# Another order for the opening of a two-layer hybrid backbone on one core

## The reference

```python
mod_l = (jax.nn.silu(c) @ w_mod[l] + b_mod[l])[:, None, :]
mod_c = (jax.nn.silu(c_ctx) @ w_mod[l] + b_mod[l])[None, None, :]
sh1, sc1, g1, sh2, sc2, g2 = jnp.split(mod_l, 6, axis=-1)
hl = modulate(rms_norm(x, norm1[l]), sh1, sc1)
hc = modulate(rms_norm(xc, norm1[l]), sh1c, sc1c)
zl = split_cols(hl @ w_in)
...
scores = jnp.einsum('bhid,bhjd->bhij', qi, ki) * decay
```

## Time and profile before

| | us |
|---|---|
| median of 3 runs | 2636.76 |
| lowest and highest | 2631.75 and 2640.86 |
| profiled execution, own time | 2634.51 |
| its span | 2632.7 |
| PE busy | 2535.3 (96%) |
| POOL busy | 1482.3 (56%) |
| DVE busy | 1365.4 (52%) |
| ACT busy | 766.4 (29%) |

### The profile page before, as it was taken

One profiled execution on the slowest core, in us unless ns is written; L12 is line 12 of the kernel. 1 busy time (PEld: TensorE's weight loads), 2 busy tenths in 40 slices (PEclk: granted clock), 3 DMA queues, 4 the chain that ended last, 5 costly groups with the idle time before them and its releaser, 6 DMA issues.

```text
span 2632.7 us, 37897 instructions
## 1 busy us (share of the span) xinstructions
PE 2535.3 (96%) x15420; PEld 2108.4 (80%) x15420; DVE 1365.4 (52%) x1855; ACT 766.4 (29%) x1292; POOL 1482.3 (56%) x1375
## 2 busy tenths in 40 slices
PE   5999999999999999999999999998999999999998
PEld 2888888877777888888887889897778678888877
DVE  3632267643477867555565364327754777421241
ACT  4611333432355521111120033123432564211110
POOL 3443557523423536666669616556834445688896
PEclk8999999999999999999999999999999999999999
DMA  7342422312312833443434354222321247333332
GB/s 275 91 136 93 116 59 71 85 51 83 87 56 77 285 106 119 128 124 116 124 105 120 112 170 143 77 57 77 85 57 53 72 127 226 113 96 96 88 94 82
DMA packets 378211, 285.11 MB, mean 108 GB/s; under 512 B 10309, under 2 KB 338729, under 8 KB 377526
## 3 DMA queue, kind: packets, MB, share of 16 engines
q1 hardware_dynamic: 375744, 279.81, 35.4%
q10 hardware_dynamic: 1686, 2.78, 0.3%
q0 software_dynamic: 608, 0.09, 0.0%
HBM read 253.28 MB, written 29.36 MB: 107 GB/s over the span
## 4 chain that ended last, share of the span: by engine, by line
PE 84%; DVE 6%; POOL 4%; ACT 2%; issue 1%; DMA 1%; ACTq 0%; SPq 0%; DVEq 0%; POOLq 0%
PE ps L561 19%; PE ps L563 18%; PE ps L562 18%; PE ps L1272 3%; PE ps L774 3%; POOL w_lo L1426 2%; PE ps L610 2%; PE ps L1204 2%; PE ps L611 2%; PE ps L612 2%; PE ps L858 2%; PE ps L878 2%; POOL w_hi L1423 1%; PE ps L984 1%; PE ps L805 1%
## 5 line engine op out<-in xcount | busy, mean ns | idle before, releaser
L1423 POOL TENSOR_TENSOR w_hi<-ring,tiny 128x512 fp32r<-128x512 f32 x480 | 536.6, 1118 | 942.0 <-PE ps L563 559.0
L1426 POOL TENSOR_TENSOR w_lo<-ring,w_hi 128x512 fp32r<-128x512 f32 (+1 forms) x568 | 798.1, 1408 | 126.4 <-ACT w_hi L1653 88.8
L561 PE MATMUL ps<-hh,w_hi 128*128 128x512 f32 (+1 forms) x2320 | 839.7, 362 | 15.4 <-DVE hl L2155 10.4
L562 PE MATMUL ps<-hl,w_hi 128*128 128x512 f32 (+1 forms) x2320 | 818.1, 353 | 0.0
L563 PE MATMUL ps<-hh,w_lo 128*128 128x512 f32 (+1 forms) x2320 | 817.4, 352 | 0.0
L561 PEld LDWEIGHTS ps<-hh,w_hi 128*128 128x128 f32 x2320 | 441.0, 190 | 107.8 <-issue 26.3
L563 PEld LDWEIGHTS ps<-hh,w_lo 128*128 128x128 f32 x2320 | 441.0, 190 | 60.8
L562 PEld LDWEIGHTS ps<-hl,w_hi 128*128 128x128 f32 x2320 | 441.9, 190 | 55.3
L1958 ACT ACTIVATE arena<-ps,vec 128x768 f32<-128x768 f32 (+1 forms) x44 | 39.0, 887 | 424.8 <-PE ps L563 424.8
L1772 ACT ACTIVATE arena<-ps,tiny,vec 128x768 f32<-128x768 f32 (+1 forms) x120 | 108.6, 906 | 184.0 <-DVE tiny L2333 183.9
L2609 DVE SCALAR_TENSOR_TENSOR arena<-ps,vec,arena 128x511 f32<-128x511 f32 x66 | 43.6, 660 | 220.5 <-ACT arena L1958 219.7
(11 more groups left out here) (274 smaller groups left out, 3814.4 us busy)
## 6 DMA issues: line engine op xcount, KB each, us to landing
ring<-in_w_in SPq DMA_DIRECT2D x118, 512.0 KB, 4.0
ring<-in_w_mod SPq DMA_DIRECT2D x96, 512.0 KB, 3.9
ring<-in_w_up SPq DMA_DIRECT2D x88, 512.0 KB, 4.2
ring<-in_w_down SPq DMA_DIRECT2D x48, 512.0 KB, 3.6
ring<-in_w_out SPq DMA_DIRECT2D x32, 512.0 KB, 3.7
logits<-arena SPq DMA_DIRECT2D x32, 384.0 KB, 2.6
arena<-logits SPq DMA_DIRECT2D x32, 384.0 KB, 4.5
ring<-in_w_down SPq DMA_DIRECT2D x24, 384.0 KB, 3.2
```

The source lines that it names most:

```text
L561: pe.matmul(acc, wh[:, offset + k], hi[:, n, x:y], start=n == 0, stop=False)
L562: pe.matmul(acc, wh[:, offset + k], lo[:, n, x:y], start=False, stop=False)
L1423: pool.tensor_tensor(wh[:, 0:count], w, one[:].unsqueeze(2).to_broadcast([P, count, P]), ALU.mult).then_inc(*up("w_lead", ("lead", key, j)))
L1426: pool.tensor_tensor(wl[:, 0:count], w, wh[:, 0:count].bitcast(F32), ALU.subtract).then_inc(*up("w_split", ("split", key, j)))
```

## The change

It changes the order of the opening and of the retention branch of layer 0, and nothing that is computed:

1. ACT computes the conditioning vectors before it squares the tokens. One load of an activation table falls away with that.
2. PE multiplies the slices of groups 0 and 1 without a break, then turns `xn` 0 and 1, then group 2, the columns of groups 0 and 1, `xn` 2 and 3, group 3, the column of group 2, `xn` 4 to 7, and the column of group 3.
3. `f0` and `f1` are computed together (`opening_features`): for each operand tile PE first turns block `x` `k`, then multiplies the tile with the weights of both.
4. In the list of chunks `f1` follows `f0` at once, and the slices that stood between them come later.
5. DVE makes a rotation as soon as its feature tile is out, and strip 0 behind rotation 1, strip 1 behind rotation 2, strips 2 and 3 behind rotation 3. ACT takes the exponentials of strip 0 behind the copy of `f2`, those of strips 1, 2 and 3 behind the copy of `f3`.

```diff
 def slices_behind(l, b, slot):
     groups = columns_between(l)[b]
-    if b == "ret" and slot >= 3:
-        slot = {3: 2 * len(groups), 4: 3}.get(slot, slot)
+    if b == "ret":
+        slot = slot - 1 if slot > 0 else 2 * len(groups)
...
+            def opening_features(*places):
+                keys = [("f", 0, "ret", n) for n in range(2)]
+                for key, place in zip(keys, places):
+                    next_chunk(key)
+                    for s, n in room(key, *place):
+                        pe.wait_ge(s, n)
+                for k in range(KT):
+                    j, offset = k // (KT // 2), k % (KT // 2)
+                    turn_tokens("x", k)
+                    pe.wait_ge(*at(("hl", 0, 1, k)))
+                    for key in keys:
+                        pe.wait_ge(*at(("split", key, j)))
+                        for x, y in segs(T):
+                            mm = product(psum(key)[:, x:y], key, j, hh, hl, x, y, count=1, first=k, offset=offset)
...
                 if l == 0:
-                    for g in range(4):
+                    for g in range(2):
                         for kk in range(4):
                             modulation_slices(("msl", l, g, kk))
-                            if kk % 2 == 1:
-                                turn_tokens("xn", 2 * g + kk // 2)
...
+                    for k in range(2):
+                        turn_tokens("xn", k)
+                    for kk in range(4):
+                        modulation_slices(("msl", l, 2, kk))
+                    for g in range(2):
+                        modulation_turned(g)
+                    for k in range(2, 4):
+                        turn_tokens("xn", k)
+                    for kk in range(4):
+                        modulation_slices(("msl", l, 3, kk))
+                    modulation_turned(2)
+                    for k in range(4, KT):
+                        turn_tokens("xn", k)
                     modulation_turned(3)
...
+            conditions()
             for t in range(NT):
                 act.wait_ge(*at(("x_in", t)))
...
-                if t == 3:
-                    conditions()
...
-                        if l == 0 and b == "ret" and j < 4:
-                            strip_exponentials(l, j)
+                        if l == 0 and b == "ret" and 2 <= j <= 3:
+                            for h in ((0,), (1, 2, 3))[j - 2]:
+                                strip_exponentials(l, h)
...
                 if b == "ret":
                     for n in range(tiles):
                         turn_halves(n)
+                        for h in ((), (0,), (1,), (2, 3))[n] if l == 0 else ():
+                            strip_begun(l, h)
+                            strip_ended(l, h)
...
-                    if b == "ret" and l == 0:
-                        for h in range(4):
-                            strip_begun(l, h)
-                            strip_ended(l, h)
```

More of the change, by code:

```diff
@@ L563, in product @@
                     mm = pe.matmul(acc, wl[:, offset + k], hi[:, n, x:y], start=False, stop=n == whole - 1)
-                    if each and key == ("f", 0, "ret", 0):
-                        turn_tokens("x", n)
-                return mm
+                return mm
+            def opening_features(*places):
[12 more added lines that the diff above has]
+                            mm = product(psum(key)[:, x:y], key, j, hh, hl, x, y, count=1, first=k, offset=offset)
+                        if offset == KT // 2 - 1:
+                            mm.then_inc(*up("pe_half", ("half", key, j), *([("full", key)] if j else [])))
             def projection(key, hi, lo, width, banks, each=None):
@@ L1081, in behind, with banks @@
                         modulation_slices(key)
-                def banks(b):
+                def banks(b, j=None):
                     turn[0] += 1
+                    if l == 0 and b == "ret":
+                        return ((2, 3), (0, 1), (4, 5), (0, 1))[j]
                     return (0, 1) if turn[0] % 2 == (b != "ret" or l > 0) else (2, 3)
@@ L1093, in _ @@
                             each = None
-                            if b == "ret" and j == 0:
-                                each = lambda k: ("hl", l, 1, "first", k) if l else ("hl", l, 1, k)
+                            if b == "ret" and j == 0 and l > 0:
+                                each = lambda k: ("hl", l, 1, "first", k)
                             if b == "ret" and j == BR[b]["nq"] and l > 0:
@@ L1098, in _ @@
                             n = feature_order(b)[j]
-                            projection(("f", l, b, n), hh, hl, W[l] if is_q(b, n) else T, banks(b), each=each)
+                            if l > 0 or b != "ret" or j >= 2:
+                                projection(("f", l, b, n), hh, hl, W[l] if is_q(b, n) else T, banks(b, j), each=each)
+                            elif j == 0:
+                                opening_features(banks(b, 0), banks(b, 1))
                             if b == "ret" and j == 0 and l > 0:
@@ L2034, in decays_and_lambdas @@
                     link(dve.tensor_scalar(onorm[:, 1, l], onorm[:, 1, l], 1.0 - init, None, ALU.mult))
+            vectors_out(2)
+            vectors_out(3)
             for k in range(1, KT, 2):
@@ L2198, in norm, with strip_begun, strip_ended @@
                 rest(KT - 1)
+            def strip_begun(l, h):
+                D = dist[:, 0:NEAR]
+                dve.wait_ge(*at(("dist_in",)))
+                dve.tensor_scalar(e0, D, 0.0, lg[:, 8 * l + h:8 * l + h + 1], ALU.max, ALU.mult)
+                dve.tensor_scalar(e1, D, 0.0, lg[:, 8 * l + 4 + h:8 * l + 5 + h], ALU.min, ALU.mult).then_inc(
+                    *up("strip_in", ("strip_in", l, h)))
+            def strip_ended(l, h):
+                D = dist[:, 0:NEAR]
+                dve.wait_ge(*at(("strip_exp", l, h)))
+                link(dve.scalar_tensor_tensor(out=strip[:, h, 0:NEAR], in0=D, scalar=0.0, in1=e0, op0=ALU.is_ge, op1=ALU.mult))
+                link(dve.scalar_tensor_tensor(out=e1, in0=D, scalar=0.0, in1=e1, op0=ALU.is_le, op1=ALU.mult))
+                link(dve.tensor_tensor(strip[:, h, 0:NEAR], strip[:, h, 0:NEAR], e1, ALU.add))
+                link(dve.tensor_tensor(strip[:, h, NEAR:], strip[:, h, NEAR:], e2, ALU.add))
             def prep_tiles(l, b):
```

59 lines of the change are left out of this document (24 added, 35 removed).

## The result

The changed kernel takes **2645.51 us** (median of 11 runs, 2641.51 to 2656.20), the kernel before 2636.76 in the same series: ratio 1.0040, 95% interval 1.0027 to 1.0053. It is slower by about 9 us. Forecast was 2640, range 2630 to 2648: the time lies in the range, but on the upper side, and past the 0.3% (2644.7) that the forecast had drawn as the bound of "slower", to which it gave 0.21; the interval of the ratio includes that bound.

A forecast was written before the change was run, and what follows sets the result against it. PE, busy 96% of the span, was taken as the bound; 12.1 us won before `f2` are lost waiting behind the strips, plus 1.7 and 2.0 for the clock: 2636.76 + 3.7 is 2640 us, range 2630 to 2648.

The forecast's parts named there:

- slower: Whole kernel: measured time over 2644.7 us, beyond the 0.3% (7.9 us) told from no change; chance 0.21.
- the long stop: Second pair of value chunks: PE waits 13.8 us for ACT's copy of the values, plus 2.0 us for the fallen clock.

The follow-up runs named there:

- e1b: Changed kernel with ACT's third set of strip exponentials behind the columns of the first value pair's place, the fourth behind the next; 2629.1 us, ratio 0.9978.
- e3: Changed kernel with the earlier kernel's order of strips on DVE and ACT, so the opening's edits alone; 2636.5 us, ratio 0.9998 to the kernel before.
- e5: Kernel before with only the first two feature tiles computed together, conditions, slices and strips as before; 2636.7 us, ratio 1.0005.
- e9: e3's kernel with ACT's second set of exponentials behind the third copy and the last two sets behind the fourth; 2628.6 us, ratio 0.9976.
- e6: e1b's kernel with DVE's first strip ended behind the fourth rotation instead of ahead of the third, other strips following; 2629.1 us, ratio 0.9972.
- e7: Changed kernel with only the fourth set of exponentials moved behind the copies of the first value pair; 2638.0 us, ratio 1.0003 to the kernel before.
- e8: Changed kernel with strips put between copies and rotations on DVE, exponentials behind second copy, fourth copy and first pair's values; 2628.7 us, ratio 0.9971.

## What to carry to other kernels

An engine's queue is in order: an instruction that waits for another engine blocks all that stands behind it. Before moving such a chain, look for copies behind it that free PSUM for TensorE, and put these first; here moving two sets of exponentials behind two copies turned 9 us lost into 7 us won (e1b). A gain in the opening is only worth what the next engine's queue can follow: cost each part with the order of its neighbours (e3, e5 and the changed kernel each bring nothing or a loss, e9 and e1b bring 7 us with the same opening). Where two parts of a change are meant to go together, time each alone as well.

## What the runs showed of the hardware

VectorE and GpSimd slow each other, both by about the same: with strips of 896 columns beside splits of 512, 1.09 became 1.65 to 2.04 on VectorE, and 1.05 and 1.27 became 1.89 and 1.99 on GpSimd. The Trainium skill (SBUF — State Buffer, SBUF: two separate sides) speaks of an exclusive lock. The trace agrees in part: both engines pay, but no strip instruction took as long as one of each in a row (2.06 at most, in e1b, where 1.09 and 1.27 add up to 2.36). Whether the lock is held for less than the whole instruction, or the two overlap at their ends, no run here shows.

Short stops of TensorE had unlike consequences at the same place. One of 1.0 us was followed by no loss of clock (the changed kernel, 1.00 in all windows from 98 to 112.5), one of 0.4 (e6) neither; 1.2 (e7), 1.6 (e8) and 2.4 us (e1b) were followed by stretches at 0.50. At another place, at the fourth feature tile (92.8 to 94.7 us), stops of 1.1 to 1.2 us (e3, e5, e9) were followed by 1.00. The windows behind e7's stop:

```profile
102.50:105.00 2.50, 2.50 (x14) 2.50 (x14) 2.46 (x2) 0.61 (x4) 2.42 (x2) 0.50 0.85 328
105.00:107.50 2.50, 2.50 (x21) 2.50 (x21) 2.47 (x3) 0.00 (x0) 2.42 (x3) 0.94 0.36 88
```

At half rate these two windows alone lose 2.5 x 0.50 + 2.5 x 0.06 = 1.4 us: a stop of 1.2 us cost more behind it than in itself. I had reckoned with that only at the long stop.
